# A hybrid mixer trunk on one core: turned rows over two banks, a gate made tile by tile, other copy marks and fill steps

## The reference

```python
for l in range(DEPTH):                       # DEPTH = 2
    h = _rmsnorm(x, norm_g[l])
    p = h @ w_in[l]                          # 1024 x 8904 columns
    ...
    oa = _chunk_band_attention(aq, ak, av, a_rel_bias[l]) * silu(az)      # A: banded attention
    ob = _hgrn2(bq, bf, bi, lb_all[l], b_norm_g[l]) * silu(bz)            # B: gated linear recurrence
    oc = _dsa(rope(cq), rope(ck), cv, rope(cqi), rope(cki), cwi) * silu(cz)  # C: top-256 keys by an indexer
    od = _rwkv7(dr, dk, dv, dwd, dad, ...) * silu(dz)                     # D: delta-rule state
    ga, gb, gc, gd = split(pg)
    y = (sigmoid(ga) * (oa @ w_branch[l, 0]) + sigmoid(gb) * (ob @ w_branch[l, 1])
         + sigmoid(gc) * (oc @ w_branch[l, 2]) + sigmoid(gd) * (od @ w_branch[l, 3]))
    x = x + y @ w_out[l]
return _rmsnorm(x, final_g)
```

## Time and profile before

| | us |
|---|---|
| Three runs, median (lowest to highest) | 2999.27 (2998.98 to 3001.17) |
| The profiled execution | 3003.82 |
| Its span, first to last instruction | 3001.9 |
| TensorE busy in it | 2865.5 |
| VectorE, ScalarE, GpSimd busy | 1558.8, 960.4, 804.6 |
| Mean granted TensorE clock (of 1) | 0.987 |

### The profile page before, as it was taken

How to read it: one execution, slowest core, us unless ns; L and a number is a source line. 1 busy time by engine, 2 the same in 40 slices (tenths; PEclk the granted TensorE clock), 3 DMA queues, 4 the chain that set the end, 5 groups by cost and what they waited for, 6 DMA issues and landing times. The chain is left out here.

```text
span 3001.9 us, 46549 instructions
## 1 busy us (share of the span) xinstructions
PE 2865.5 (95%) x18816; PEld 1538.1 (51%) x18816; DVE 1558.8 (52%) x3143; ACT 960.4 (32%) x1820; POOL 804.6 (27%) x572
## 2 busy tenths in 40 slices
PE   8999999999999999999999999999999999999998
PEld 4546454575544465544445464545755444754443
DVE  3587757533358812165236877585333597030643
ACT  2355653211133325300113556633111423253001
POOL 2036313302233232232020452133022322322320
PEclk9999999999999999999999999999999999999999
DMA  6112101101121221263051211011011112212731
GB/s 230 32 43 57 43 18 53 43 16 41 37 78 36 79 94 53 95 213 109 0 163 27 60 45 36 26 46 43 19 42 47 67 47 80 81 46 96 230 98 56
DMA packets 134988, 204.64 MB, mean 68 GB/s; under 512 B 8920, under 2 KB 88952, under 8 KB 134008
## 3 DMA queue, kind: packets, MB, share of 16 engines
q1 hardware_dynamic: 116184, 167.59, 17.7%
q10 hardware_dynamic: 18592, 34.09, 3.1%
HBM read 146.07 MB, written 48.78 MB: 65 GB/s over the span
## 5 line engine op out<-in xcount | busy, mean ns | idle before, releaser
L500 PE MATMUL ps<-hT,wr 128*128 128x512 f32 x1600 | 749.8, 604 | 0.1
L500 PEld LDWEIGHTS ps<-hT,wr 128*128 128x128 f32 x1600 | 290.0, 191 | 304.9 <-issue 293.4
L500 PE MATMUL ps<-sums,wr 128*128 128x512 f32 x800 | 387.4, 613 | 7.0 <-ACT gts L570 4.5
L651 POOL TENSOR_TENSOR gts<-gts,wr 128x512 f32<-128x512 f32 x96 | 136.1, 1417 | 635.9 <-ACT wr L551 485.2
L500 PEld LDWEIGHTS ps<-sums,wr 128*128 128x128 f32 x800 | 147.1, 195 | 160.5 <-issue 146.4
L729 PE MATMUL ps<-xo,arena 128*128 128x512 f32 x512 | 220.1, 592 | 0.0
L626 POOL TENSOR_TENSOR wr<-wr 128x512 f32<-128x512 f32 (+1 forms) x56 | 87.4, 1561 | 438.6 <-PE ps L500 322.2
L1129 DVE CUSTOM_DVE_ANT_0 arena<-ps,arena 128x640 f32<-128x640 f32 (+7 forms) x128 | 90.4, 706 | 219.6 <-PE ps L1030 201.7
L500 PE MATMUL ps<-wr 128*128 128x512 f32 x400 | 193.3, 607 | 7.2 <-ACT wr L551 7.2
L1497 DVE TENSOR_SCALAR_CACHE_REDUCE arena<-arena,sm 128x384 f32<-128x384 uint16 (+7 forms) x256 | 192.8, 810 | 2.2
L551 ACT ACTIVATE wr<-ps 128x512 f32<-128x512 f32 x150 | 88.9, 593 | 301.3 <-PE ps L500 281.4
(11 more groups left out here) (313 smaller groups left out, 4666.2 us busy)
## 6 DMA issues: line engine op xcount, KB each, us to landing
wr<-in_w_in SPq DMA_DIRECT2D x68, 1024.0 KB, 5.3
gate_tanh<-gts ACTq DMA_DIRECT2D x128, 256.0 KB, 2.1
arena<-gate_tanh SPq DMA_DIRECT2D x128, 256.0 KB, 3.0
x_cur<-arena SPq DMA_DIRECT2D x2, 4096.0 KB, 23.9
arena<-in_w_branch SPq DMA_DIRECT2D x8, 1024.0 KB, 9.5
wr<-in_w_out SPq DMA_DIRECT2D x8, 1024.0 KB, 7.1
arena<-x_cur SPq DMA_DIRECT2D x4, 2048.0 KB, 8.8
arena<-arena SPq DMA_DIRECT2D x36, 128.0 KB, 2.9
```

The costliest lines, as they stand in the source:

```text
L500: ins = pe.matmul(ap, lhsT=right(u, w_side)[:, kt, :], rhs=left(h_side, kt), start=fresh and kt == 0, stop=kt == half_k - 1, skip_group_ch ...
L651: pool.tensor_tensor(dst, dst, stage_of(u), ALU.add).then_inc(sg("pool_added"), 1)
```

## The change

- Turned rows of B go to bank T and bank O by turns, where all went to T.
- A's gate is made tile by tile: Tanh of one 128x256 tile by ScalarE in the second of each four attention units, and its product by VectorE in the third. Before its attention A does 54 fill steps, where it went on until the unit was complete. A separate flag (`masked`) now says where C's masks have to be waited for.
- B's first steps are four groups of 12 with four marks, where there were three of 16; ScalarE copies up to the second mark between its logarithms. The steps at "end", "khn" and the fourth "adds" are 8, 3 and 13 in the first of two rounds, where they were 6, 2 and 11; in the second round they are 6, 2, 13 and then 1, where they were 6, 2, 11 and then 3. A new mark lies after four of the eight "turn" steps, and ScalarE copies up to it before it waits for the sum of squares.
- Steps: 185 beside the search (181), 28 before D's bonus (37).

```diff
-TOPK_FILL = 181
+A_FILL = 54
+TOPK_FILL = 185
...
-D_FILL = {"start": 6, "kk": 19, "bonus": 37, "decay": 10, ...
-B_FILL = {"start": 16, "end": 6, "khn": 2, "adds": (3, 3, 3, 11, 3), "att": 1, "last": 2, "turn": 8}
+D_FILL = {"start": 6, "kk": 19, "bonus": 28, "decay": 10, ...
+B_FILL = {"start": 12, "end": (8, 6), "khn": (3, 2), "adds": (3, 3, 3, 13, 1), "att": 1, "last": 2, "turn": 8}
...
             def pe_o_turn(pe, b, i, og):
-                ap = jobs.open(pe, key, T)
+                ap = jobs.open(pe, key, O if b == "B" and i % 2 else T)
...
                 att = attention("A", q, k, v, z, lambda i: max(0, i - BAND + 1),
-                                lambda i, h, nb: bias8[:, h, P * (BAND - nb):P * BAND], 12, (14, 15, 16), ("A", 1))
+                                lambda i, h, nb: bias8[:, h, P * (BAND - nb):P * BAND], 12, (14, 15, 16), ("A", 1),
+                                each_unit=lambda dve, u: dve_gate(dve, u // 4) if u % 4 == 2 else None,
+                                act_unit=lambda act, u: act_gate(act, u // 4) if u % 4 == 1 else None)
+                def act_gate(act, i):
+                    if i == 0:
+                        unit_done(act, ("A", 1))
+                    act.activation(z_tanh[:, i % 2, :], z[:, i, :], ACT.Tanh, scale=0.5).then_inc(sg("z_tanh_A"), 1)
+                def dve_gate(dve, i):
+                    dve.wait_ge(sg("z_tanh_A"), i + 1)
+                    link(dve, dve.scalar_tensor_tensor(z[:, i, :], z_tanh[:, i % 2, :], 1.0, z[:, i, :], ALU.add, ALU.mult))
...
                 def pe(pe):
-                    pe_fill_until(pe, ("fills", "A"), ("A", 1))
+                    pe_fill(pe, A_FILL)
+                    jobs.mark(("fills", "A"))
...
                     act_fills(act, ("fills", "A"))
-                    unit_done(act, ("A", 1))
-                    act.activation(z_tanh, H(2, 2), ACT.Tanh, scale=0.5).then_inc(sg("z_tanh_A"), 1)
                     att[1](act)
...
-                    dve.wait_ge(sg("z_tanh_A"), 1)
-                    link(dve, dve.scalar_tensor_tensor(H(2, 2), z_tanh, 1.0, H(2, 2), ALU.add, ALU.mult))
+                    link(dve, ins)
...
-                    for n in range(3):
+                    for n in range(4):
                         pe_fill(pe, B_FILL["start"])
                         jobs.mark(("B start", n))
...
-                        pe_fill(pe, B_FILL["khn"])
+                        pe_fill(pe, B_FILL["khn"][m])
...
-                    pe_fill(pe, B_FILL["turn"])
+                    pe_fill(pe, B_FILL["turn"] // 2)
+                    jobs.mark("B turn")
+                    pe_fill(pe, B_FILL["turn"] // 2)
...
                     act.activation(two, bc_flat, ACT.Ln, bias=1.0)
+                    act_fills(act, ("B start", 1))
...
-                    act_fills(act, ("B start", 2))
+                    act_fills(act, ("B start", 3))
...
+                    act_fills(act, "B turn")
                     act.wait_ge(sg("b_square"), 1)
```

More of the change, by code:

```diff
@@ L50 @@
 FIRST_T = {"t1": 1, "t2": 2, "t3": 3, "t4": 4}
-D_FILL = {"start": 6, "kk": 19, "bonus": 37, "decay": 10, "CH": 2, "Y": 1, "X": 2, "UZ": 1, "P": 1, "S": 1, "norm": 12, "turn": 24}
-B_FILL = {"start": 16, "end": 6, "khn": 2, "adds": (3, 3, 3, 11, 3), "att": 1, "last": 2, "turn": 8}
+D_FILL = {"start": 6, "kk": 19, "bonus": 28, "decay": 10, "CH": 2, "Y": 1, "X": 2, "UZ": 1, "P": 1, "S": 1, "norm": 12, "turn": 24}
+B_FILL = {"start": 12, "end": (8, 6), "khn": (3, 2), "adds": (3, 3, 3, 13, 1), "att": 1, "last": 2, "turn": 8}
 FILL_ORDER = [("D", (0,)), ("D", (4,)), ("C", (4,)), ("C", (5,)), ("C", (2, 3)), ("D", (1,)), ("D", (2,)), ("D", (3,)), ("B", (0,)), ("B", (3,)),
@@ L992, in gated_merge_kernel, with attention @@
             MIX = {}
-            def attention(b, q, k, v, z, first_tile, bias, at_s, at_pt, v_unit=None, each_unit=None, act_unit=None):
+            def attention(b, q, k, v, z, first_tile, bias, at_s, at_pt, v_unit=None, each_unit=None, act_unit=None, masked=False):
                 units = [(i, h) for i in range(NT) for h in range(4)]
@@ L1123, in dve @@
                             ap = jobs.ready(dve, ("S", b, u))
-                            if each_unit is not None and h == 0 and i >= 2:
+                            if masked and h == 0 and i >= 2:
                                 dve.wait_ge(sg("masks_made"), i - 1)
@@ L1160, in mixer_a @@
                 mask = H(10.5, 0.625)
-                z_tanh = H(12, 2)
+                z_tanh = H(21.25, 0.5).rearrange("p (n c) -> p n c", n=2)
                 toep_l = nc.dram_tensor(f"toep_l{l}", [4, 768], F32, kind="Internal").ap()
@@ L1264, in select_ahead @@
                     select(dve, u // 4 + 2, u % 4)
-                att = attention("C", q, k, v, z, lambda i: 0, bias, 10, (17.25, 18.25, 9), ("C", 2), each_unit=select_ahead, act_unit=make_mask)
+                att = attention("C", q, k, v, z, lambda i: 0, bias, 10, (17.25, 18.25, 9), ("C", 2), each_unit=select_ahead, act_unit=make_mask, masked=True)
                 roped = [("ki", ki, 0, 0)] + [("qi0", qi, m, m) for m in (0, 1)] + [("qi1", qi, m, m + 2) for m in (0, 1)]
@@ L1555, in pe @@
                     for m in range(2):
-                        pe_fill(pe, B_FILL["end"] // 2)
+                        pe_fill(pe, B_FILL["end"][m] // 2)
                         jobs.mark(("B end", m, 0))
-                        pe_fill(pe, B_FILL["end"] // 2)
+                        pe_fill(pe, B_FILL["end"][m] // 2)
                         jobs.mark(("B end", m, 1))
```

## The result

The changed kernel took 2982.18 us (median of five runs, 2979.49 to 2986.85) against 2999.20 us (2998.03 to 3001.17) before: a ratio of 0.9947, 95% interval 0.9936 to 0.9957. It is faster, by 17.0 us. The prediction was 2967 us, a gain of 31.8 us. The time lies inside the range of 2955 to 2984 us, but the gain is only a little over half of the one forecast.

What follows compares the result with a forecast made beforehand. TensorE was taken as the bound, busy 2865.5 of 3001.9 us, so only its idle time and low-clock time could move. Terms summed to -15.9 us a layer, -31.8 for two: 2999.27 - 31.8 = 2967 us, range 2955 to 2984.

Steps and rivals of the forecast that it cites:

- search, 185 steps: C's start: four more steps fill TensorE's wait for exponentials, -3.4 us a layer, and regain clock behind it, -1.0.
- D's bonus, 28 steps: Ahead of D's bonus: new wait for r*k, +4.4 us, and slow clock, +1.5 (0 to +2.5); +5.9 a layer.
- B up to its first states: B's start: four waits shrink or go, one new wait of +0.9; together -4.0 us a layer (-4.9 to -1.5).
- "turn" mark: B's turn steps: earlier ScalarE copy removes a 2.26 us wait and 1.8 of slow clock, -4.1 us a layer.
- two banks, with the clock behind: B's turned rows: eight turns shorten from 7.9 to 3.9 us, -4.0 a layer, and clock behind them, -1.7.
- A's gate: Ahead of A's first scores: wait of 1.91 us and slow clock go, -3.6 us a layer (-3.6 to -1.5).
- Nothing behind it gets later: Behind D's bonus: VectorE's next step starts 3.3 us sooner, so no further delay was counted.
- rival (1): B's turned rows: two banks bring nothing because ScalarE's copies set the pace; 2979 us, chance 0.14.
- (2): B's start: VectorE keeps the pace, so the -4.0 shrinks to about -1; 2973 us, chance 0.14.
- (3): D, C, B and behind the turns: open prices all come out at their good ends; 2960 us, chance 0.10.
- (4): Behind D's bonus: half clock through 30 decay steps, +24 us a layer, slower at 3012 us; chance 0.04.
- (5): Whole kernel: no change, since steps are conserved and the waits only move; chance 0.06.

Runs made afterwards that it cites:

- steps only: Kernel before with only step numbers changed: 185 beside the search (181), 28 ahead of D's bonus (37); 3012.29 us, ratio 1.0040.
- both late parts: Kernel before with only B's turned rows on two banks and A's gate tile by tile (54 steps ahead of A's attention); 2979.76 us, ratio 0.9936.
- the other pair of runs: Changed kernel with a 28-step merge gate unit ahead of B's turned rows, 28 against 37 steps ahead of D's bonus: 2979.55 against 2958.87 us.
- the run with 37 steps: Changed kernel with 37 steps ahead of D's bonus in place of 28; 2984.03 us, ratio 0.9949.

## Why the prediction was wrong

The direction, the places and most terms were right. In us over both layers, the forecast's term and what the runs gave:

| part | forecast | measured | from |
|---|---|---|---|
| search, 185 steps | -8.8 | -6.4 | search only |
| D's bonus, 28 steps | +11.8 | +19.3 | steps only, less the search |
| B up to its first states | -8.0 | -4.5 | what the others leave of -17.0 |
| "turn" mark | -8.2 | -5.6 | changed kernel without it |
| two banks, with the clock behind | -11.4 | -13.5 | two banks only |
| A's gate | -7.2 | -6.3 | both late parts, less the banks |
| sum | -31.8 | -17.0 | |

These differences were measured in different kernels, and the line of B is only what the others leave, not a run.

- **The step that failed is D's part, "+5.9" a layer; it cost 9.7, and 10.3 by the other pair of runs.** The wait came out (4.4, measured 4.58), but partly by luck: the product r*k, for which it waits, took 3.35 us beside a GpSimd addition where it had taken 2.28, and with the additions cut the wait is 3.5. The clock was mis-sized: +1.5 was taken, with a bound of 2.5, and the bonus alone took 2.45 longer (6.99 against 4.54). The two pieces behind it ran at half clock as well, about as long as before. From the start of the bonus to D's first copies the changed kernel lost 3.0 us against the one profile of before (it was 4.90 us ahead at the bonus and 1.89 at the transposes of v). And 1.9 us were in no term: the wait for D's gated rows, 1.52, and one for a copy among them, 0.40. 4.6 + 3.0 + 1.9 = 9.5.
- **"Nothing behind it gets later" was wrong, because the sum has no term for GpSimd.** Pieces that move carry GpSimd's additions and sums of weights with them. In D's last eight products VectorE's rows are stretched from 2.29 us to 3.24 in five cases and 2.96 in one, against three of 3.24 before, so D's rows come 1.7 us later although D began earlier.
- **B's turned rows took back 1.15 us a layer.** I had read that TensorE came to the turns without waiting but not how long before that VectorE had been ready: 5.2 us. Of my terms only the turn mark's 4.1 counts against that, since VectorE's chain starts with the end of the attention, and 4.1 would have fitted. The product's 2.0 us more took the slack below it: 5.2 less 2.0 and 4.1 leaves TensorE about 1 us early, and it waits 1.15. A cheaper D that does not take steps from B's end would have moved the gated rows as well; no run has that, so what it would have given stays open.
- **The search** gave 3.2 a layer instead of 4.4: the wait went from 3.89 to 1.07, not 0.5, and 1.0 was lost again at D's sum of squares. Both are VectorE beside GpSimd once more. The exponential came 0.6 later because a copy of VectorE just ahead of it took 1.19 us in place of 0.57, beside a sum of weights (the copy before, and after the change); and the product ahead of the sum of squares took 3.23 in place of 2.29.

```profile
352.35 0.57 DVE L1515 COPY arena<-con 128x128 f32<-128x128 f32 x1
```

```profile
350.07 1.19 DVE L1525 COPY arena<-con 128x128 f32<-128x128 f32 x1
349.92 1.27 POOL L630 TENSOR_TENSOR wr<-wr 128x512 f32<-128x512 f32 x1
```

- **B's start** came out as forecast in the trace: from D's first turned row to the end of the attention the changed kernel takes 154.8 us (881.94 to 1036.71) and the one before 154.6 (881.55 to 1036.15), with five steps (4.3 us) more in it, so 4.1 a layer is saved. The -4.5 of the table is thus too small by what the other lines carry of scatter. One reading in the prediction was off: the 2.9 us of L1573 in the earlier trace rows are four waits, two a layer, so that 5.5 us stood there and not 4.9. Of them 0.6 a layer is left (L1583), and the only new wait is 0.45 us (0.9 forecast); the table loads between the logarithms show no wait.
- **The turn mark** removed its wait of 2.26 and gave the clock back, as forecast, and made VectorE's product 2 us longer: ScalarE's earlier copies let GpSimd's additions start beside it. In the run without the mark the first layer's product is at 2.36 us.
- **Two banks and A's gate** came out as forecast, in the trace and in the time. The section of the Trainium skill that spoke for rival (1) ("TensorE: Matmul & The Clock Gate", "HAM oscillation — how this bites in real kernels") does not carry over: here the second bank gave 13.5 us.

Rivals (2) to (5) did not happen as described; (2) named VectorE as the one who keeps the pace, but at B's beginning, and not at D's end and B's end.

## What to carry to other kernels

A wait that is not in the trace has a slack: before adding up savings on one engine, read at each place where it meets another engine how much earlier that one was ready, and what had released that one. Savings between the release and the meeting count only up to the slack; savings ahead of the release move both engines; savings behind the meeting count in full, and here they were the whole gain. Where filler work is moved, what it sets off on other engines moves too: look which of their instructions then come to lie beside each other. And work that is pulled forward is missing as cover at the next point that runs only to the end of its unit.

## What the runs showed of the hardware

- The same VectorE product of two on-chip operands took 2.29 us or up to 3.39 (128x2048), and the pair of 128x1024 took 2.36, 4.38, 5.46 or 6.52 us, by what GpSimd did beside it; with GpSimd's additions cut it was 2.37. What decides is which of the two began first. Of the 88 products of 128x2048 in the profiles of before and after, 31 ran clear of GpSimd's instructions and took 2.28 to 2.29 us; 27 began before the GpSimd instruction beside them and took 2.28 to 2.30 as well; 28 began while one of GpSimd's was running and took 2.79 to 3.39; two began in the last 0.1 us of one and took 2.29. Where VectorE was first, GpSimd's instruction was the one that took longer: 3.18 us at 1045.92, beside a product begun at 1045.68, against 1.26 for an addition of the same size at 352.88 (the profile's times of GpSimd are rough). The Trainium skill, "SBUF — State Buffer", section "SBUF: two separate sides", says that the two engines share one pair of ports, which the instruction that starts first holds as a whole while the other is blocked. The trace agrees in these counts, and in the run with 37 steps GpSimd was busy for all of the 6.52 us.
- A wait of 3.5 to 4.6 us ahead of the thin bonus went with a half-clock stretch of 10 to 14 us in each run that had it, part of it within the wait; with a wait of 1.16 us or none the stretch was 0 to 6.8 us.
- The runs of the changed kernel spread over 7.4 us and those of before over 3.1. The mean granted clock of the five varies from 0.989 to 0.992 with the span (2985.1 to 2977.7 us). Up to 3.6 us of such differences arise ahead of the first search, which VectorE begins 191.7 to 195.3 us after the start in the profiles with full additions, though the code up to there is the same. Why one execution has fewer low stretches than the next stays open.
